# Layer 0 of a hybrid streaming encoder: modulation as columns, x transposed on TensorE beside the low-rank projection

## The reference

```python
cs = jax.nn.silu(c)
for l in range(DEPTH):
    mod = cs @ w_mod[l] + b_mod[l]                 # (B, 3D)
    shift, scale, gate = jnp.split(mod[:, None, :], 3, axis=-1)
    h = rmsnorm(x, g_pre[l]) * (1 + scale) + shift
    z = h @ w_in                                   # even layers
    cq, ckv, kr, bq, bk, bv, gate = jnp.split(z, [o1, o2, o3, o4, o5, o6], axis=-1)
    q = (rmsnorm(cq, g_q) @ w_uq) ...
    ...
    x = x + gate * rmsnorm(y, g_post[l])
```

## Time and profile before

| what | value |
|---|---|
| median of 3 runs | 4604.71 us (4601.04 to 4605.65) |
| the profiled execution's own time | 4598.65 us |
| its span on the slowest core (core 3) | 4597.1 us |
| spans of the eight cores | 4562.9 to 4597.1 us |
| TensorE busy, share of the span | 93% |
| first 188 us of the span | TensorE busy 17 us |

### The profile page before, as it was taken

The page is one execution under the profiler, slowest core; times in us unless marked ns, Lnnn a source line. Parts: engine busy times, 40 slices in busy tenths (PEclk is TensorE's granted clock), DMA queues, the critical chain, the costliest instruction groups (busy, mean ns, idle before and its releaser), DMA issues.

```text
span 4597.1 us, 80959 instructions; the slowest of 8 cores (4562.9 to 4597.1 us)
## 1 busy us (share of the span) xinstructions
PE 4287.5 (93%) x30884; PEld 2429.7 (53%) x30884; DVE 1788.2 (39%) x3725; ACT 1186.8 (26%) x2187; POOL 458.1 (10%) x482
## 2 busy tenths in 40 slices
PE   0388999999999899999999899999999999999998
PEld 0146767667744345444444567767774444544444
DVE  0563442333356326111475444233335733510133
ACT  1124443222223123000232344322223322300011
POOL 1021010000000001222002101000000000122200
PEclk9989999999999999999999999999999999999999
DMA  9977775454585787457767556545438566523544
GB/s 200 167 141 111 114 101 73 62 68 51 72 223 188 165 171 195 76 92 101 200 191 128 86 92 91 73 61 68 49 56 223 192 147 157 142 37 47 91 156 138
DMA packets 666891, 550.93 MB, mean 120 GB/s; under 512 B 416352, under 2 KB 602976, under 8 KB 647568
## 3 DMA queue, kind: packets, MB, share of 16 engines
q0 software_dynamic: 321760, 239.09, 37.3%
q1 hardware_dynamic: 344752, 306.65, 23.9%
HBM read 620.54 MB, written 100.76 MB: 157 GB/s over the span
## 4 chain that ended last, share of the span: by engine, by line
PE 84%; DMA 6%; DVE 3%; another core or an unknown queue 2%; issue 2%; SPq 1%; ACT 1%; POOL 0%; DVEq 0%; ACTq 0%; POOLq 0%
PE PS L300 81%; PE PS L298 4%; DMA RG<-R 1%; DMA W<-sg_w_in 1%; SPq L337 1%; DVE R L325 1%; DMA RG<-w_mod 1%; DVE R L322 1%; DMA RG<-ab_w_out 1%; DMA VR<-R 1%; DMA R<-tb 1%; DVE RG L319 0%; DMA W<-g_post 0%; ACT R L310 0%
## 5 line engine op out<-in xcount | busy, mean ns | idle before, releaser
L300 PE MATMUL PS<-RG,W 128*128 128x512 bf16 x6528 | 1501.8, 380 | 43.4 <-DMA RG<-R 18.5
L300 PE MATMUL PS<-W,RG 128*128 128x128 bf16 (+3 forms) x13952 | 1499.0, 262 | 44.2 <-DVE R L325 21.4
L310 ACT ACTIVATE R<-PS 128x512 bf16<-128x512 f32 (+5 forms) x1536 | 777.6, 515 | 2335.8 <-PE PS L300 1558.8
L300 PEld LDWEIGHTS PS<-W,RG 128*128 128x128 bf16 x13952 | 1047.3, 98 | 529.2 <-issue 80.2
L300 PEld LDWEIGHTS PS<-RG,W 128*128 128x128 bf16 x6528 | 631.6, 98 | 777.2 <-issue 83.9
L300 PE MATMUL PS<-RG 128*128 128x512 bf16 (+2 forms) x3968 | 960.1, 375 | 8.2 <-DMA RG<-ab_w_out 5.9
L300 PEld LDWEIGHTS PS<-RG 128*128 128x128 bf16 x3968 | 388.9, 98 | 397.8 <-issue 15.0
L300 PE MATMUL PS<-R 128*128 128x512 bf16 (+3 forms) x1604 | 393.5, 295 | 5.4 <-DVE R L319 3.8
L310 ACT ACTIVATE RG<-PS 128x2048 bf16<-128x2048 f32 (+2 forms) x128 | 151.5, 1184 | 870.8 <-PE PS L300 862.9
L325 DVE CAST R<-PS 128x512 bf16<-128x512 f32 (+1 forms) x352 | 233.6, 667 | 352.5 <-PE PS L300 269.3
L322 DVE TENSOR_TENSOR RG<-PS,R 128x512 bf16<-128x512 f32 x128 | 88.5, 691 | 708.6 <-PE PS L300 707.9
(11 more groups left out here) (79 smaller groups left out, 1946.0 us busy)
## 6 DMA issues: line engine op xcount, KB each, us to landing
W<-w_mod POOLq DMA_DIRECT2D x64, 1024.0 KB, 9.9
RG<-w_mod POOLq DMA_DIRECT2D x32, 1024.0 KB, 16.5
W<-ab_w_in POOLq DMA_DIRECT2D x64, 512.0 KB, 8.4
VR<-R SPq DMA_DIRECT2D x128, 256.0 KB, 4.1
R<-VR SPq DMA_DIRECT2D x32, 1024.0 KB, 6.2
W<-sg_w_in POOLq DMA_DIRECT2D x32, 1024.0 KB, 13.4
XB<-R SPq DMA_DIRECT2D x20, 1024.0 KB, 6.9
RG<-XB SPq DMA_DIRECT2D x20, 1024.0 KB, 6.2
```

Source lines behind the costliest of these rows:

```text
L300: P.op("pe", lambda e: e.matmul(o, lhsT, rhs, start=start, stop=stop), r=r, w=w, sig=sig)
L310: P.op("act", lambda e: e.activation(out=o, in_=i, func=func, **kw), r=r, w=w, wp=wp)
```

## The change

`startup` is rewritten; everything behind it keeps its order.

- Modulation as columns. The slab now is the stationary operand: for each slab 32 matmuls, each with 128 x 128 slab values as weights and one column of the conditioning vector moving, add into 16 columns of a PSUM bank (bank 6 for scale, 7 for shift). DVE adds the bias and, for scale, makes `(1 + scale) * g_pre`, on tiles of 128 x 16 (`ab_t`: A and B with the channel on the partition). The bias and `g_pre` come as columns with a new input `mcol`. `MODROW` and the repeated read are no longer used for shift and scale of layer 0.
- x. Four tiles are loaded at the start and scaled (ACT square, DVE multiply by the reciprocal norm alone, in place, fp32) in the middle of the modulation. Tiles 4 to 7 are loaded when the fifteenth slab has landed, the others two at a time at the end of each pair's turn. Tiles are scaled one pair ahead of their use.
- Transposes. For each pair of tiles there are 8 turns. A turn transposes 2 channel blocks of 2 tiles on PE (4 `transpose` of 128 x 128 fp32, with the tile as the stationary operand and an identity moving) into one of banks 0 to 5. Then the bank is evacuated by two instructions of 128 x 256, which multiply by A and add B with the channel on the partition, write bf16, and are on DVE and ACT by turns.
- cq beside it. The 32 matmuls of the pair before are dealt out, four after each turn, into banks 6 and 7; there are 9 rounds, the first with transposes only and the last with cq only. The normalized cq is staged in `W` blocks 16 to 21, not in RG1.
- `WCQ` is loaded after the twelfth slab. The other low-rank weights stay behind the last slab.

```diff
+            def cols(k):
+                _, third, s = mq[k]
+                buf, toks = mbuf(k)
+                b = 7 - third
+                bv = buf.rearrange("p (k c) -> p k c", c=2048)
+                for q in range(2):
+                    for m in range(16):
+                        mm(bank(b)[:, m:m + 1], bv[:, q, m * 128:(m + 1) * 128], csc[:, 2 * s + q:2 * s + q + 1], s == 0 and q == 0 and m == 0,
+                           s == 7 and q == 1, r=toks + RT(2, 1), w=[PS_t[b]], sig=(q == 1 and m == 15), skip=True)
...
-            for t in range(8):
+            for t in range(NP):
                 loadx(t)
...
+                ts("dve", x, x, rs, None, ALU.mult, None, r=xt + s_, w=xt)
...
             for k in range(16):
-                mod_mm(*mq[k], *mbuf(k), nb(), Wf(24, 2), WT(24, 2))
-                if k == 7:
-                    dma("sp", Rf(A_KB, 8), rep_row(MODROW[0, 1]), r=[MR_t[0][1]], w=RT(A_KB, 8))
+                cols(k)
+                if k in (7, 15):
+                    o, third = (A, 1) if k == 7 else (B, 0)
+                    tt("dve", o, bank(7 - third)[:, 0:16], mc[:, 16 * (1 - third):16 * (2 - third)], ALU.add, r=[PS_t[7 - third]] + RT(1, 1), w=[ab_tok[third]])
...
+                if k == 3:
+                    wload(WCQ, ab_w_in[0, :, 0:512], RT(28, 16))
+                if k == 8:
+                    for t in range(NP):
+                        scale(t)
+            after = mbuf(14)[1][:1]
+            for t in range(NP, 8):
+                loadx(t, after)
...
+                        P.op("pe", lambda e, o=o, src=src: e.transpose(o, src, ident), r=xt + RT(0, 1), w=[PS_t[b]], sig=(q == 1 and i == 1))
...
+                    if ev["k"] % 2:
+                        act(o, i_, AF.Identity, r=[PS_t[b]] + ab_tok, w=w, bias=B[:, kc:kc + 1], scale=A[:, kc:kc + 1])
+                    else:
+                        ts("dve", o, i_, A[:, kc:kc + 1], B[:, kc:kc + 1], ALU.mult, ALU.add, r=[PS_t[b]] + ab_tok, w=w)
...
+            for p in range(9):
+                if p == 2:
+                    load_lowrank_rest(0)
...
+                for j in range(8):
+                    if p < 8:
+                        turn(p, j)
+                    if j in (2, 4) and NP <= 2 * p + 1 + j // 2 < 16:
+                        scale(2 * p + 1 + j // 2)
+                    if p:
+                        c = c0 if j < 4 else c1
+                        for _ in range(4):
+                            c[0].pop(0)()
+                        if not c[0]:
+                            c[1]()
+                if 1 <= p < 5:
+                    loadx(2 * p + 6)
+                    loadx(2 * p + 7)
```

More of the change, by code:

```diff
@@ L243, in build @@
         ccol_t = sb("ccol_t", [128, 16], F32)
+        ab_t = sb("ab_t", [128, 32], F32)
         P = Prog(nc, es)
@@ L254, in build @@
         acc_t = Tok("acc")
+        ab_tok = [Tok("ab%d" % i) for i in range(2)]
         st_t = [Tok("st%d" % i) for i in range(8)]
@@ L510, in load_lowrank_rest, with cq_tile @@
                     a_w_uq[i, kc * 128:(kc + 1) * 128, :].rearrange("p (h c) -> p h c", c=192)[:, :, 128:192], w=WT(12 + kc, 1))
-        def cq_tile(t, hr, yr, wcq, wcqt, late=None):
-            b = nb()
-            for kc in range(16):
-                mm(bank(b), G[hr][:, kc, tile(t)], wcq[:, kc, :], kc == 0, kc == 15, r=[GT[hr][kc][t]] + wcqt(kc), w=[PS_t[b]], sig=(kc == 15))
+        def cq_tile(t, hr, yr, wcq, wcqt, late=None, split=False):
+            b = 6 + t % 2 if split else nb()
             k = t % 6
@@ L519, in cq_tile, with one, rest @@
             sgt = gt(yr, [ch], range(4 * q, 4 * q + 4))
[L520 to L523 removed]
+            if split:
+                sg, sgt = Wb(16 + k, 1), WT(16 + k, 1)
+            def one(kc):
+                mm(bank(b), G[hr][:, kc, tile(t)], wcq[:, kc, :], kc == 0, kc == 15, r=[GT[hr][kc][t]] + wcqt(kc), w=[PS_t[b]], sig=(kc == 15))
             def put():
                 dmaT(G[yr][:, 12:16, tile(t)], sg, r=sgt, w=gt(yr, range(12, 16), [t]))
[L527 to L530 removed]
+            def rest():
+                c, s_ = newst()
+                act(sg, bank(b), AF.Square, r=[PS_t[b]], w=s_ + sgt, accum=st[:, c:c + 1])
+                rs = rstd_of(c, s_, 512)
+                stt("dve", sg, bank(b), rs, Wf(28, 2), ALU.mult, ALU.mult, r=[PS_t[b]] + s_ + WT(28, 2), w=sgt)
+                if late is not None and t >= 12:
+                    late.append(put)
+                else:
+                    put()
+            ms = [lambda kc=kc: one(kc) for kc in range(16)]
+            if split:
+                return ms, rest
+            for f in ms:
+                f()
+            rest()
         def ckv_pass(hr, yr):
```

81 lines of the change are left out of this document (44 added, 37 removed).

## The result

The changed kernel takes 4565.1 us (median) against 4604.4 for the kernel before: a ratio of 0.9913 with a 95% interval of 0.9893 to 0.9932, about 39 us. A second series of the same kernel gave 0.992 (0.9905 to 0.9935). Ratios, intervals and ranges of runs leave out executions in which the cores of a die ran at a lower granted clock throughout (here one of four, at 5260.8 us).

What follows compares the result with a forecast made beforehand. Transfers were taken to bound the start up to the last slab, PE the rounds behind it. Cq ending at 255.6 instead of 278.5 gave -22.9, plus 2.5 given back: -20.4 us, so 4584.3 us, range 4572 to 4617.

Steps and rivals of the forecast that it cites:

- given back behind: Behind cq: attention weights now load beside the rotary tables and POOL's arithmetic waits behind issues; 2.5 us lost, 0 to 5.
- The last slab: End of the modulation's slab transfers: last slab's columns start at 161 us (157 to 166), 3 us worse than before.
- three strips gone: Transfers ahead of the last slab: bias rows no longer read, priced like one x tile, -2 us.
- read of A gone: Transfers ahead of the last slab: A no longer read back repeated on 128 partitions, priced like one x tile, -2 us.
- WCQ ahead of four slabs: WCQ's load now precedes the last four slabs; before, it landed 11.4 us behind the last slab: +11.4 us.
- the 8.4 us between slabs: Interval between landings of the other twelve slabs before the change, taken as showing a stretch bound by transfers.
- The columns: 32 one-column matmuls on PE behind the last slab: 4.0 us, between 2.2 and 6.5; earlier slabs' columns hidden.
- The rounds: Transposes and cq per pair of x tiles, bound by PE: 11.2 us a round (10.2 to 12.5), seven make 78.4.
- The 0.8 a round: In each mixed round, one evacuation on DVE or ACT added to PE's 10.4 us, giving 11.2.
- Rival 1: Slow fp32 transposes in the rounds: gain gone at 0.18 us each, 4616.5 us total at 0.226; chance 0.22.
- Rival 2: PE's clock falls in the rounds because transposes don't keep it up; at half clock +32 us, 4637; chance 0.07.
- Rival 3: Gain mostly lost behind cq to late attention weights and POOL holding up `ckv_pass`: 10 to 20 us, about 4600; chance 0.09.

Runs made afterwards that it cites:

- the second execution: The changed kernel profiled once more, nothing altered: last slab at 139.4 us, `ckv_pass` at 233.1 (means over the cores), ratio 0.992 to the kernel before.

## Why the prediction was wrong, point by point

| step | forecast | measured (slowest core) |
|---|---|---|
| last slab's columns start | 161 (157 to 166) | 142.96 |
| the 32 columns | 4.0 | 0.85 to the first transpose |
| first round | 5 | 5.84 |
| a transpose in the rounds | 0.10 | 0.1075 (four per turn, 0.43 us apart from the cq matmul behind them) |
| seven rounds | 78.4 | 78.3 |
| last round | 7.2 | 7.8 |
| cq ends | 255.6 | 235.7 |
| given back behind | 2.5 | 2.75 (the wait behind `ckv_pass`: 12.99, before 10.24) |

**The last slab** is the step that failed, by 18 us, which is nearly the whole 19 us between the forecast of 20.4 and the measured 39. Its terms, in us that the last slab moves:

| term | forecast | measured |
|---|---|---|
| three strips gone | -2 | -10 to -14 |
| read of A gone | -2 | -4 to -5 |
| four x tiles fewer at the start | -8.8 | -10.5 to -12.1 |
| x tiles 4 to 7 beside the last slab | +3.7 | +1.3 to +1.8 |
| WCQ ahead of four slabs | +11.4 | +15 to +17 |

The measured terms are those of the experiments above and add up to -8 to -15; in the mean over the cores the last slab moved by -12 and, in the second execution, -14. "I price the last two like an x tile each, 4 us" is the sentence that was most wrong: the strips and the read of A were worth 14 to 19. The step priced each transfer by its bytes. What a strip costs those who wait behind it is what it puts on the few parts of each slab that share its way: four of sixteen came late. WCQ was priced too low, and the other four terms moved the opposite way by more. That the slabs gain just about what the strips alone cost is a coincidence, as the other four measured terms nearly cancel.

The prediction also took the 8.4 us between slabs for the speed of the transfers. A look at what the queue had moved in that time, the bytes of five slabs for four that became usable, would have shown that the interval was not bandwidth. With 6.3 us in place of 8.4 its own formula gives 3.4 us an x tile (measured 2.6 to 3.0), and not 2.2. Its lower end, 157, was too high for the same reason: it let some effects be nothing, but none be larger than its bytes.

**The columns** cost less than the lower end of 2.2: one moving column takes 0.03 us (32 in 0.99), while the nearest row had 128 columns.

**The rounds** came out to 0.1 us, but not by their parts, so the closeness is luck. PE was the bound as said, and a turn without a wait takes 1.30 us, 10.4 a round as forecast. The 0.8 a round that was added for evacuations on DVE or ACT covers, as it happens, one wait of 2.58 us for late x tiles and some 0.5 in each later round. A steady round, in the columns of the windows above:

```profile
205.00:216.00 11.00, 10.65 (x66) 6.89 (x65) 8.50 (x18) 9.60 (x21) 0.00 (x0) 1.00 0.76 176
```

The scaling by one factor took DVE 1.29 instead of the upper price of 2.35, but its evacuations took 0.54 instead of 0.43, and ACT's 0.56 instead of 0.39, in the form with a scale and an offset. ACT was thus second at 9.6 a round, and not DVE. The rows by form (busy us, mean ns) from 143 to 236 us of the changed kernel, beside the earlier trace rows:

```profile
L321 DVE TENSOR_SCALAR RG<-PS,ab_t 128x256 bf16<-128x256 f32 x64 | 31.5, 537 | 11.1 <-DMA RG<-x 6.6 <-PE PS L1395 4.5
L319 DVE TENSOR_SCALAR RG<-RG,st 128x2048 f32<-128x2048 f32 x12 | 15.4, 1286 | 1.3
...
L315 ACT ACTIVATE RG<-PS,ab_t 128x256 bf16<-128x256 f32 x64 | 31.8, 557 | 115.8 <-PE PS L1395 115.8
```

"Loads of x ... I price them at nothing" was wrong once: tiles 4 and 5 came late and cost the 2.58 us.

**Rival 1**, slow transposes: no. T is 0.1075, close to a weight load, and not 0.226. Its price of 2.56 us for each 0.01 was a little high; doubling gave 20.6 to 21.1 for 0.1075, 1.9 to 2.0 for 0.01, as waits take up the first 6 us.

**Rival 2**, the clock: no. The granted clock is 1.00 (2.4 GHz) in every mixed round and with twice the transposes. The Trainium skill (TensorE: Matmul & The Clock Gate, Part 4: PE-mode transpose) states that the full clock does not engage for transposes. This case does not agree: the spacing of transposes fell from 0.21 to 0.11 us in the middle of a run of nothing else.

**Rival 3**, the gain given back: hardly at this place. `ckv_pass` took 51.0 us, forecast 50.5. At the end of the wait behind it PE is 40.3 us ahead (315.48 against 355.77); the spans of the slowest cores differ by 33.1 in these two executions and the medians by 39.3. In the mean over the cores, 39.4 us early at the end of that wait became 33.1 at the end in this execution, 43.9 became 39.8 in the second. So 4 to 6 us are given back later: 2 to 3 of them by 460 us in both, and in the first execution some 4 more between 1600 and 2240. What makes it is open. It may also be why the strips put back cost 9 to 11 us at `ckv_pass` and 6 to 10 in the total.

## What to carry to other kernels

Price a DMA that runs beside others by the load on its busiest engine, not by its bytes: look at its outermost dimension, and if small reads run beside large ones, lay them out on 128 rows or split them, as the two kernels with the strips on 128 rows and in four DMAs did, and see in the trace whether the parts of a large load then come together. Before an interval between landings is taken for bandwidth, compare it with the bytes that the queue moved in it. And look for work that needs no late operand and can run early. Here scaling under the slabs, with the transposes on PE, brought 30 us, and a second round of transposes under WCQ, with WCQ in pieces behind the slabs, another 9 at `ckv_pass`, while the faster form of the modulation brought nothing by itself.
